# Second expert layer of a two-block kernel: every other pair of tiles by a seven-product block scheme

## The reference

```python
h = gelu(einsum('thkd,td->thk', u_table[idx], xb))
return einsum('thk,thkd->td', gate * h, v_table[idx])
...
x = _layer_norm(DN_ALPHA * x + _peer(x, ...), ln2_g, ln2_b)
```

## Time and profile before

| | |
|---|---|
| median of 3 executions | 1736.15 us (1732.58 to 1736.35) |
| the profiled execution | 1735.36 us, its span 1733.6 us |
| PE busy | 1682.9 us, 97% of the span |
| DVE, ACT, POOL busy | 66%, 46%, 21% |
| the second expert layer | 1536 matmuls, about 1374 to 1725 us |
| in it, of 348.8 us | PE 348.8, DVE 157.7, ACT 136.0, POOL 197.1 us busy |
| granted TensorE clock in it | 1.00 |
| DMA in it | 0.64 of the 16 engines, 194 GB/s |

### The profile page before, as it was taken

How to read it: one execution, slowest core, us unless ns; L and a number is a source line. 1 busy time by engine, 2 the same in 40 slices (tenths; PEclk the granted TensorE clock), 3 DMA queues, 4 the chain that set the end, 5 groups by cost and what they waited for, 6 DMA issues and landing times.

```text
span 1733.6 us, 32733 instructions
## 1 busy us (share of the span) xinstructions
PE 1682.9 (97%) x12718; PEld 1498.6 (86%) x12718; DVE 1149.4 (66%) x1883; ACT 789.3 (46%) x1239; POOL 358.1 (21%) x325
## 2 busy tenths in 40 slices
PE   6999999999999999999899999999999999999997
PEld 2999769877999889878779999999999988888886
DVE  4877777687565466874664799488999644444444
ACT  4433345755454444642244534555544433333334
POOL 2000010111000010000010667500000155555554
PEclk9999999999999999999999999999999999999999
DMA  9878855436564544430044455555555566666665
GB/s 359 291 270 299 294 216 171 146 122 245 181 215 172 194 137 144 171 122 27 27 171 151 132 173 181 164 160 162 158 157 163 171 194 193 193 192 192 192 192 166
DMA packets 64960, 314.40 MB, mean 181 GB/s; under 512 B 7216, under 2 KB 7632, under 8 KB 45776
## 3 DMA queue, kind: packets, MB, share of 16 engines
q1 hardware_dynamic: 63504, 305.94, 53.3%
q10 hardware_dynamic: 1280, 6.82, 1.1%
q0 software_dynamic: 64, 0.04, 0.0%
HBM read 311.72 MB, written 1.05 MB: 180 GB/s over the span
## 4 chain that ended last, share of the span: by engine, by line
PE 89%; DVE 5%; DMA 3%; ACT 2%; issue 1%; POOL 1%; SPq 0%; DVEq 0%; POOLq 0%; ACTq 0%
PE bank L421 25%; PE bank L423 24%; PE bank L422 24%; DMA ring<-in_stream 2%; DVE ring_rounded L381 2%; PE bank L2900 2%; PE bank L2873 1%; PE bank L2459 1%; DMA ring<-in_experts 1%; PE bank L1442 1%; POOL ring_rounded L3206 1%; PE bank L853 1%; PE bank L2472 1%; ACT arena_rounded L367 1%; PE bank L2112 1%
## 5 line engine op out<-in xcount | busy, mean ns | idle before, releaser
L423 PE MATMUL bank<-yb_rounded,ring_rounded 128*128 128x256 f32 x2032 | 574.3, 283 | 0.0
L2991 ACT CAST ring_rounded<-ring 128x1024 fp32r<-128x1024 f32 x248 | 260.4, 1050 | 284.6 <-DMA ring<-in_experts 284.6
L423 PEld LDWEIGHTS bank<-yb_rounded,ring_rounded 128*128 128x128 f32 x2032 | 389.2, 192 | 0.0
L381 DVE TENSOR_TENSOR ring_rounded<-ring,arena_rounded 128x1024 fp32r<-128x1024 f32 x230 | 270.9, 1221 | 117.1 <-ACT arena_rounded L367 116.5
L421 PE MATMUL bank<-yb_rounded,arena_rounded 128*128 128x256 f32 x1104 | 315.3, 286 | 2.6 <-DVE ring_rounded L381 1.7
L422 PE MATMUL bank<-yT_rounded,arena_rounded 128*128 128x256 f32 x1104 | 312.4, 283 | 0.0
L3166 DVE TENSOR_TENSOR ring_rounded<-ring,ring_rounded 128x1024 fp32r<-128x1024 f32 x128 | 156.8, 1225 | 191.7 <-ACT ring_rounded L2991 191.7
L421 PE MATMUL bank<-yb_rounded,ring_rounded 128*128 128x256 f32 x960 | 278.0, 290 | 1.3 <-ACT field L3018 0.5
L367 ACT CAST arena_rounded<-ring 128x1024 fp32r<-128x1024 f32 x230 | 229.1, 1048 | 95.0 <-PE bank L421 88.3
L422 PE MATMUL bank<-yT_rounded,ring_rounded 128*128 128x256 f32 x960 | 271.1, 282 | 0.0
L422 PE MATMUL bank<-ring_rounded,arena_rounded 128*128 128x512 f32 x688 | 267.8, 389 | 0.0
(11 more groups left out here) (447 smaller groups left out, 2621.6 us busy)
## 6 DMA issues: line engine op xcount, KB each, us to landing
ring<-in_stream SPq DMA_DIRECT2D x140, 1024.0 KB, 4.9
ring<-in_experts SPq DMA_DIRECT2D x256, 512.0 KB, 3.6
field<-in_stream SPq DMA_DIRECT2D x28, 512.0 KB, 7.1
field<-in_stream SPq DMA_DIRECT2D x4, 1024.0 KB, 7.0
yT<-in_stream SPq DMA_DIRECT2D x4, 512.0 KB, 7.7
field<-in_gains ACTq DMA_DIRECT2D x3, 512.0 KB, 8.6
field<-in_gains ACTq DMA_DIRECT2D x1, 1536.0 KB, 6.6
const<-in_const SPq DMA_DIRECT2D x1, 1473.0 KB, 11.7
```

What stands on the lines that cost most here:

```text
L381: ins = nc.vector.tensor_tensor(ring_r[:, g % SLOTS, half], ring[:, g % SLOTS, half], top.bitcast(F32), ALU.subtract)
L423: return first, pe.matmul(bank, s_rest, m_top, start=False, stop=stop)
L2991: nc.scalar.copy(expert_top[:, n % E_SLOTS, :], expert_w[:, n % E_SLOTS, :]).then_inc(expert_top_ready, 1)
```

## The change

The first 8 tiles and the last 4 stay as they were. The 116 between are 29 rounds of four: two tiles in slots 0 and 1 as before (12 matmuls each), then the pair in slots 2 and 3 as one block product. Take the pair's `hidden` as blocks A11, A12, A21, A22 (token half, tile) and its values as B11, B12, B21, B22 (tile, output half). Instead of the eight products of 128 x 128 by 128 x 512 it makes seven, of sums of blocks:

- S1 = A21 + A22, S2 = S1 - A11, S3 = A11 - A21, S4 = A12 - S2 (POOL, four subtractions or additions of 128 x 128);
- T1 = B12 - B11, T3 = B22 - B12, T2 = B22 - T1, T4 = B21 - T2 (DVE, one of 128 x 1024 and two of 128 x 512);
- all seven pairs of factors are split into top and rest: ACT rounds A (128 x 512), S (128 x 512), B11 (128 x 512), B21 with B22 (128 x 1024), T (2 x 128 x 1024); POOL subtracts for A and S, DVE for the others.

Three products go to `four` banks, four to the `A` banks, which accumulate over all rounds and are combined once at the end. Each product is again three passes, so a pair costs 21 matmuls where it cost 24. The buffers of A, S and T have one copy each: ACT may round the next pair's A only when PE has finished this pair (`t_used`).

```diff
+            def v_pair(p1, p5, p7, p6, first_pair, last_pair):
...
+                pe.wait_ge(a_split, of_pair(pairs, 2, 1))
+                pe.wait_ge(raw_split, of_pair(pairs, 2, 1))
+                first, last = product(p1, A11, *raw(0, 0))
+                first.then_inc(expert_begun, 1)
...
+                pe.wait_ge(raw_split, of_pair(pairs, 2, 2))
+                first, _ = product(four[0], A12, *raw(1, 0), own=False)
+                first.then_inc(expert_begun, 1)
+                pe.wait_ge(a_split, of_pair(pairs, 2, 2))
+                _, last = product(four[1], S4, *raw(1, 1), own=False)
+                last.then_inc(raw_used, 1)
+                pe.wait_ge(t_split, of_pair(pairs, 2, 1))
+                first, last = product(p5, S1, *summed(T1))
+                first.then_inc(expert_begun, 1)
...
+                _, last = product(p7, S3, *summed(T3))
...
+                pe.wait_ge(t_split, of_pair(pairs, 2, 2))
+                _, last = product(p6, S2, *summed(T2))
...
+                _, last = product(four[2], A22, *summed(T4), own=False)
+                last.then_inc(t_used, 1)
...
+            def round_of_four(last_pair=False):
+                v_tile(0, begins=False)
+                v_tile(1)
+                v_pair(*of_sums, False, last_pair)
...
+            def round_act(g):
+
+                act.wait_ge(s_sum, of_pair(pairs, 4, 4))
+                if pairs.n:
+                    act.wait_ge(t_used, of_pair(pairs, 1, 0))
+                nc.scalar.copy(a_top[:, 0:512], pair_block(g)).then_inc(a_top_ready, 1)
+                nc.scalar.copy(a_top[:, 512:1024], s_plain).then_inc(a_top_ready, 1)
...
```

More of the change, by code:

```diff
@@ L2925, in peer_pe, with v_tile @@
             four = [V.take(pe) for _ in range(4)]
[L2927 to L2930, removed]
+            def v_tile(slot, first_tile=False, begins=True):
+                b = slot % 2
                 mixed.n += 1
@@ new lines, in peer_pe @@
+            for g in range(HEAD):
+                v_tile(g % E_SLOTS, first_tile=(g == 0))
+            v_tile(0)
+            v_tile(1)
+            seen["sums"] = A.filled.n
+            of_sums = [A.take(pe) for _ in range(4)]
+            v_pair(*of_sums, True, False)
+            def round_of_four(last_pair=False):
+                v_tile(0, begins=False)
+                v_tile(1)
+                v_pair(*of_sums, False, last_pair)
+            loop(pe, ROUNDS_OF_FOUR - 2, 1, lambda g, j: round_of_four(), [(mixed, 2), (pairs, 1)])
@@ new lines, in peer_dve, with added @@
+            while mixed.n < HEAD + 2:
+                v_rests(mixed.n % E_SLOTS)
+            round_dve()
+            loop(dve, ROUNDS_OF_FOUR - 1, 1, lambda g, j: round_dve(), [(pairs, 1), (mixed, 2)])
+            v_rests(2)
+            v_rests(3)
+            u1, u2, u3, u4, u5 = sums_before
+            p5, p7, p6 = [A.banks[(seen["sums"] + i) % 4][:, :] for i in (1, 2, 3)]
+            quarter = lambda t, n: xh[:, t, n * 512:(n + 1) * 512]
+            def added(ins, n):
+                ins.then_inc(sums_added, 1)
+                dve.wait_ge(sums_added, n)
@@ new lines, in with_residual @@
+            def with_residual(t, n, part):
+                return vec.scalar_tensor_tensor(quarter(t, n), quarter(t, n), ALPHA, part, ALU.mult, ALU.add)
+            dve.wait_ge(bank_copied, 1)
+            dve.wait_ge(A.done, seen["sums"] + 4)
+            vec.tensor_tensor(u2, u1, p6, ALU.add).then_inc(sums_added, 1)
+            with_residual(0, 0, u1)
+            dve.wait_ge(sums_added, 1)
+            vec.tensor_tensor(u4, u2, p5, ALU.add).then_inc(sums_added, 1)
+            vec.tensor_tensor(u3, u2, p7, ALU.add).then_inc(sums_added, 1)
@@ L3193, in peer_dve @@
                 for n in range(2):
-                    layer_sum_dve(dve, t, n, first, BY_TOKEN)
+                    dve.wait_ge(V.done, first + BY_TOKEN[t][n])
+                    vec.tensor_tensor(quarter(t, n), quarter(t, n), V.banks[(first + 2 * t + n) % 4][:, :], ALU.add
+                                      ).then_inc(sem("half_added"), 1)
+                    halves_added["dve"] += 1
+                    V.emptied.n += 1
             dve.wait_ge(sem("last_norm_in"), 16)
```

169 lines of the change are left out of this document (147 added, 22 removed).

## The result

The changed kernel takes 1849.11 us (median of 4 runs, 1848.2 to 1851.59), the kernel before 1735.34 us on the same chip (4 runs, 1732.58 to 1736.35): ratio 1.066, interval 1.064 to 1.068. It is 114 us slower. 1838 was forecast, 1795 to 1885 as the range.

What follows compares the result with a forecast made beforehand. TensorE bounds the old kernel; after the change DVE and POOL taking turns at SBUF would: 13.5 + 0.9 = 14.4 us a round against 10.88, 98.6 + 4.0 = +102.6 us on 1735.4, so 1838 us, range 1795 to 1885.

Steps and rivals of the forecast that it cites:

- TensorE's saving: TensorE, round of four tiles: 45 matmuls in place of 48, 10.20 us, 0.68 us less.
- DVE and POOL exclude each other: SBUF reads: the two engines take turns except some 0.14 us at an operation's start, 13.5 us a round together.
- The round at full clock: From pair to pair: 13.5 us of DVE and POOL turns plus 0.9 us idle, 14.4 us a round.
- a gap of 0.9: Behind POOL's fourth sum: ACT rounds A while neither DVE nor POOL uses SBUF, 0.9 us a round.
- the third landing is hidden: Slot 3's reload: lands some 4.5 us after issue, at about 9 us in a round of 14.4, before its reader.
- TensorE's second pause: Ahead of A12's product: TensorE waits 1.6 us for DVE's rest of B21 and B22.
- Rival 1: Less DVE and POOL interference; slot 3's reload chain sets rounds of 10.2 to 10.9 us, 1725 us; faster 0.06, no change 0.02.
- Rival 3: TensorE's clock falls to 1.2 GHz after pauses: up to 1887 us, 2013 if low throughout; chance 0.10 over 1885.
- The pause ahead of the pair: TensorE, before the pair's first product: a wait of 2.3 us in each round.
- The sum: Whole kernel: 28 intervals x (14.4 - 10.88) = 98.6 us, plus 4.0 for start and end, +102.6 us.
- its bounds: Round length: 13.2 to 15.5 us, from uncertain 128- and 512-element operations and a gap that could vanish.
- rivals 1 and 2: The second: operations pack better than laid out, 12 to 13.2 us a round, 1768 to 1802 us; chance 0.09.

Runs made afterwards that it cites:

- e6: Changed kernel with all sums on POOL and DVE, their roundings and rests left out from the second pair on: 1726.0 us.
- e3: Changed kernel with ACT rounding B11 and B21 with B22 ahead of A and S: 1826.1 us.
- e10: e3 with POOL's casts for a round's two plain tiles moved to ACT: 1822.0 us.
- e12: e3 with the plain tiles' casts moved to ACT and slot 3's reload waiting only for the last product of B22: 1807.8 us.
- e1: Changed kernel without POOL's four sums and its subtractions for A and S from the second pair on: 1772.2 us.
- e4: Changed kernel with twelve matmuls of zeros a round filling TensorE's waits around the pair's first product: 1837.6 us.
- e2: Changed kernel with ten memsets of 512 elements in place of POOL's sums and subtractions for the pair: 1790.1 us.

## Why the prediction was right, and which steps were not

**TensorE's saving: right.** 10.20 us a round was forecast; most rounds of e6 take 10.20.

**DVE and POOL exclude each other, at the prices forecast: right.** In the changed kernel, a DVE operation of 1024 elements that found POOL running ended 1.08 us after it (1.09 forecast), one of 512 0.547 (0.55); a POOL operation of 128 elements ended 0.32 us after DVE (0.32), one of 256 0.59 (0.60), one of 512 1.154 (1.14), a cast 0.257 (0.26). The unknown 128-element operation takes 0.460 us by itself (0.46 forecast). The rule of the page "SBUF — State Buffer", section "Who interferes with whom", in the Trainium skill holds as to who is excluded; taken for whole durations it gave 16.1 us a round, and the rounds took 14.1.

**The round at full clock: right in size, with the wrong path.** Forecast was 13.5 us of taking turns plus a gap of 0.9 in which neither engine works, behind POOL's fourth sum. The trace has that place (1431.72 to 1432.73), but DVE's L3315 runs there, because it had been late: it waited 1.14 us for slot 3's landing. So the gap was 0.4, not 0.9. What closes the round is the loop through slot 3, with 2.5 us of POOL's turns in it. The step that failed is that the third landing is hidden, about 9 us in a round of 14.4, ahead of its reader. The landing was not late (8.3 us behind p1, at 1431.62), but DVE had finished its list at 7.3 us. It waits for the landing in each of the 29 pairs, 54.9 us in all, in the changed kernel's waits:

```profile
PEld bank L421 <- issue: 78.5, 38, 4.7
PE bank L421 <- DVE ring_rounded L3323: 63.9, 29, 4.3
DVE const L3315 <- DMA ring<-in_experts: 54.9, 29, 3.1
```

TensorE's second pause, ahead of A12's product, was 0.65 us in most rounds, where 1.6 was forecast.

Whether that loop or the turns would have to be shortened first in the changed order itself was not tried; on e3's order, e10 to e12 show three paths (POOL's list, slot 3's loop, DVE's list) within 0.6 us of each other (13.7, 13.6 and 13.2). That the forecast of the one came out close to the time of the other is probably due to this closeness; it was not foreseen, and so it is luck.

**Rival 1: its time was wrong, whatever POOL does.** It gave 10.2 to 10.9 us for slot 3's loop without disturbance, and 1725 us. (Its terms add up to 10.0 to 10.2.) e1 shows 11.71 us, 11.2 without the stretching that is left: the landing took 4.14 us there and 4.5 in the median of e1's rounds, in place of 3.6 to 3.8, though the prediction's own paragraph on DMA had 4.5 for the third. And between the rests of B and the reload stand six matmuls, their start and p5's first, 1.9 us, where I had put one rest of T, 1.2. With that number the loop alone is over the 10.88 us of before, and the 0.08 that the rival held for no loss had nothing to stand on.

**Rival 3: partly true, and to be added, not chosen.** I had left the clock out of the likeliest sum. The pause ahead of the pair was 2.3 us in the median, as laid out (0.7 to 2.8 from round to round), 21 of the 28 rounds had stretches at 0.50, and the clock over the rounds was 0.89, under the 0.95 that was named as this rival's sign. They make the average round 14.75 in place of 14.1, 18 us in all. e4, in which they don't occur from the second round on, is 11.5 us faster by the medians, to which the matmuls of zeros themselves add 28 x 0.16 = 4.5: 16 us, and some 2.7 more were lost in its first round. Near enough. For a clock that stays low the prediction took 0.453 us a matmul, twice 0.227; in the stretch of the earlier trace rows they start 0.43 us apart.

**The sum.** 28 x (14.75 - 10.88) = 108.4 us against 98.6 forecast: 28 x 0.3 = 8.4 less from rounds of 14.1 in place of 14.4, and 28 x 0.65 = 18.2 more from the clock. Around the rounds, the span shows 116.2 - 108.4 = 7.8 us against 4.0. The first pair waited 4.4 us in place of 2.8 (p1 at 1408.53, tile 9 begun at 1401.39 and 2.72 long), and the nine tiles begun from 1375.51 up to 1401.39 took 2.75 to 2.98 us each in place of 2.72, 1.4 us together, which I can't explain: in e3, with the same head, they take 2.72. The stage also began 1.1 us later than before (1375.51 against 1374.43), ahead of all that the change touches. The profiled execution was the slowest of the four, 2.5 us over their median, so these last two need not stand in the others.

So it is luck as well that 1838 came within 14 us of the profiled 1851.6: 8 us too much for the round at full clock stand against 18 too little for the clock and 4 too little around the rounds. Two sums in the prediction do not come out: its bounds add up to 12.9 to 16.2 us a round, where it says 13.2 to 15.5, and rivals 1 and 2 leave out the 4.0 us for start and end. The round measured, 14.1 or 14.75, lies inside either.

## What to carry to other kernels

Price a saving on the busiest engine against every loop that the new preparation closes (operation, product, reload, landing, operation), with the landing and the matmuls in it, not only against the sum of work on the engines: here seven products for eight saved 0.68 us a round, and the loop alone, undisturbed, took 11.2 us, 0.3 more than the old round. Where DVE reads two operands from SBUF and POOL reads SBUF too, their times add nearly in full (here 1.08 of 1.22 us and 1.15 of 1.29), so POOL is no free place for such sums. When two paths are close, mending one of them shows almost nothing (4 and 6 us), and both together much more (18).

## What the runs showed of the hardware

- POOL's memset of 512 elements takes 526 ns and does not lengthen DVE's operations beside it (692 ns for 512 elements, 1225 for 1024); POOL's sums and subtractions do (1671 for L3318 and 1518 for L3315 in the changed kernel, 692 and 1226 for the same two lines in e2).
- A pause of some 2.3 us was followed by a fall of the clock in some rounds and not in others: the round from 1423.33 us began after a pause of 2.46 us and stayed at 1.00, the next began after 2.33 us and had 3.4 us at 0.50. So the 2.2 us of the earlier trace rows, which the prediction called enough for a fall, were not enough each time. DVE and POOL keep their prices in the rounds with stretches at 0.50 (a DVE operation of 1024 elements ends 1.08 us after POOL's in all of them), and the second of these rounds took 0.8 us more (14.84 against 14.06) for 3.4 us at half clock, since TensorE has waits to give.
- Where slots 1, 2 and 3 are asked for close together, the first load of 512 KB took 3.5 us from issue to landing in the median of the changed kernel's rounds, as alone (3.6), the second 4.4 and the third 4.3 (3.6 to 5.1).
